# Moving one expert's scatter matmuls within the expert loop of a sparse mixture-of-experts stage

## What is computed

```
gate = ...                      # [256 tokens, 16 experts], two entries of a row are not zero
out = zeros_like(t)             # t: [256, 1024]
for e in range(16):
    hid = silu(t @ w1[e]) * (t @ w3[e])      # w1, w3: [1024, 512]
    out = out + gate[:, e:e+1] * (hid @ w2[e])   # w2: [512, 1024]
```

## Time and profile before

| what | value |
|---|---|
| median of 3 runs | 1847.81 us (1847.75 to 1850.71) |
| the profiled execution's own time | 1842.55 us |
| its span, first to last instruction | 1840.6 us |
| the expert loop in it | about 1494 to 1829 us |
| one pass of the loop | 20.97 us |

### The profile page before, as it was taken

How to read it: one execution, slowest core, us unless ns; L and a number is a source line. 1 busy time by engine, 2 the same in 40 slices (tenths; PEclk the granted TensorE clock), 3 DMA queues, 4 the chain that set the end, 5 groups by cost and what they waited for, 6 DMA issues and landing times.

```text
span 1840.6 us, 20850 instructions
## 1 busy us (share of the span) xinstructions
PE 1717.3 (93%) x8330; PEld 1370.4 (74%) x8330; DVE 1145.0 (62%) x1626; ACT 900.1 (49%) x1380; POOL 39.3 (2%) x45
## 2 busy tenths in 40 slices
PE   7999999999999999899999999979899879999997
PEld 7987886768887898697676788737658557777776
DVE  7366656565555836665756545554644378888887
ACT  5476433434443548543333444242532257777774
POOL 0010000000000001000000000001000000000000
PEclk9999999999999999999999999999956889999999
DMA  6454234446553545424554555362400248887885
GB/s 262 160 190 153 92 140 158 183 160 241 191 186 137 205 139 205 160 92 155 191 192 160 195 187 189 132 270 78 168 1 28 72 180 299 307 306 294 302 294 188
DMA packets 48746, 333.18 MB, mean 181 GB/s; under 512 B 6146, under 2 KB 6788, under 8 KB 9860
## 3 DMA queue, kind: packets, MB, share of 16 engines
q1 hardware_dynamic: 48644, 331.79, 49.0%
HBM read 330.72 MB, written 1.05 MB: 180 GB/s over the span
## 4 chain that ended last, share of the span: by engine, by line
PE 74%; DVE 15%; ACT 7%; DMA 2%; issue 1%; POOL 1%; DVEq 0%; SPq 0%; ACTq 0%
PE bank L192 71%; DVE wls L204 6%; PE bank L196 3%; ACT whs L200 2%; DMA raw<-in_ws_dram 2%; DVE arena L204 1%; DVE tail L209 1%; ACT tail L200 1%; DVE P0l L204 1%; ACT P0h L200 1%; DVE more L204 1%; ACT arena L201 1%; POOL sm L224 1%; ACT arena L200 1%; DVE arena L713 1%
## 5 line engine op out<-in xcount | busy, mean ns | idle before, releaser
L204 DVE TENSOR_TENSOR wls<-raw,whs 128x1024 fp32r<-128x1024 f32 x500 | 593.6, 1227 | 298.8 <-ACT whs L200 298.6
L200 ACT ACTIVATE whs<-raw 128x1024 fp32r<-128x1024 f32 x500 | 502.7, 1051 | 276.7 <-PE bank L192 197.0
L192 PE MATMUL bank<-whs,P0h 128*128 128x512 f32 (+1 forms) x1104 | 438.5, 397 | 29.1 <-DVE P0l L204 19.5
L192 PE MATMUL bank<-whs,P0l 128*128 128x512 f32 (+1 forms) x1104 | 429.3, 389 | 0.0
L192 PE MATMUL bank<-wls,P0h 128*128 128x512 f32 (+1 forms) x1104 | 428.6, 388 | 0.0
L192 PEld LDWEIGHTS bank<-whs,P0h 128*128 128x128 f32 x1104 | 208.9, 189 | 79.4 <-DVE P0l L204 22.8
L192 PEld LDWEIGHTS bank<-whs,P0l 128*128 128x128 f32 x1104 | 208.6, 189 | 44.1
L192 PEld LDWEIGHTS bank<-wls,P0h 128*128 128x128 f32 x1104 | 209.2, 189 | 40.0
L192 PE MATMUL bank<-whs,P1h 128*128 128x512 f32 x400 | 160.9, 402 | 6.1 <-DVE P1l L204 5.4
L192 PE MATMUL bank<-P0h,whs 128*128 128x256 f32 x512 | 148.5, 290 | 10.2 <-DVE P0l L204 6.1
L192 PE MATMUL bank<-whs,P1l 128*128 128x512 f32 x400 | 157.5, 394 | 0.0
(11 more groups left out here) (185 smaller groups left out, 1879.4 us busy)
## 6 DMA issues: line engine op xcount, KB each, us to landing
raw<-in_ws_dram SPq DMA_DIRECT2D x302, 1024.0 KB, 4.8
lnb<-in_ln_g_dram SPq DMA_DIRECT2D x6, 512.0 KB, 5.7
lnb<-in_ln_b_dram SPq DMA_DIRECT2D x6, 512.0 KB, 6.6
tail<-in_bias_dram SPq DMA_DIRECT2D x1, 2048.0 KB, 7.6
h<-in_x_dram SPq DMA_DIRECT2D x2, 512.0 KB, 3.9
lnb<-in_mem_dram SPq DMA_DIRECT2D x1, 1024.0 KB, 12.6
memT<-in_ctx_dram SPq DMA_DIRECT2D x1, 1024.0 KB, 7.0
lnb<-in_b_ada_dram SPq DMA_DIRECT2D x2, 512.0 KB, 9.6
```

The costliest lines, as they stand in the source:

```text
L192: return PE.put(lambda e: e.matmul(out, lhsT, rhs, start=start, stop=stop, skip_group_check=skip), w, inc)
L200: return AC.put(lambda e: e.activation(out, in_, func, bias=bias, scale=scale), w)
L204: return VE.put(lambda e: e.tensor_tensor(out, a, b, op), w)
```

## The change

The call `scatter(e - 1)` is moved from behind `down(e, 1)` to between `down(e, 0)` and `turn_hidden(e, 1)`. Nothing is added or taken away; for e = 0 there is no such call.

```
@@ expert loop @@
                 up(e, 1)
                 feed(1)
                 down(e, 0)
+                if e:
+                    scatter(e - 1)
                 turn_hidden(e, 1)
                 feed(1)
                 if e + 1 < NEXP:
                     pick(e + 1)
                 feed(1)
                 down(e, 1)
                 feed(1)
-                if e:
-                    scatter(e - 1)
                 if e + 1 < NEXP:
                     turn_onehot(e + 1)
```

## The result

The changed kernel is slower: 1858.76 us median (1856.81 to 1866.56, 6 runs) against 1847.76 us before (6 runs), a ratio of 1.0081 with a 95% interval of 1.0063 to 1.0099. (The ratio is that of the comparison of the timed runs and not the quotient of the two medians, which lie 11.0 us or 0.6% apart; 1.0081 is 15.0 us on 1847.76. The ratios further down are of the same kind, each against its own runs of the kernel before.) The forecast was 1851.0 us in a range of 1846.3 to 1856, within 0.2% of before the likeliest. The time lies outside the range, and a wait that the prediction doesn't name made it so.

The account below looks back on a forecast made before the run. PE bounds the loop, with DVE having only some 2.5 us to spare. Terms -3.5 + 3.5 + 2.4 + 0.8 = +3.2 us on 1842.55 us profiled, plus 5.3 to the median, gave 1851.0 us, range 1846.3 to 1856.

Parts of the forecast that it names:

- Term 1: PE's wait for P0l ahead of the second down product, counted from T (chunk 1 transposes' start), shrinks 0.25 us: -3.5 us.
- Term 2: New wait ahead of the next expert's u1 matmuls, 0.17 us idle plus 0.08 restart, 14 times: +3.5 us.
- Term 3: d0's landing delays P0l of chunk 0 and the next first down product, 0.17 us in 14 passes: +2.4 us.
- rival C: Slower: d0's landing at ACT's F3' lacks cover; 1854.5 us at 5.1 us, 1860.1 at 5.5; chance 0.23.
- Term 4: In the last pass the previous expert's scatter no longer covers part of the last Y split: +0.8 us.
- B: Gain without new waits: u1 closed by T + 7.65, only term 1 and the end count, 1845.1 us; chance 0.12.
- D: No visible effect: terms 1 and 2 cancel, landing 0.1 early, only the end counts, 1848.6 us; chance 0.15.

Follow-up runs that it names:

- the first experiment: Changed kernel with the first up product in PSUM bank 6 instead of bank 4 and the one-hot work in bank 7; ratio 1.0057 to the kernel before.
- after_swap: Changed kernel with the second down product making its two column halves in the order 1, 0; ratio 1.0221 to the kernel before.
- half: Kernel before with only the first 4 of the 8 scatter matmuls moved ahead of the chunk 1 transposes; ratio 1.0012.
- mid: Kernel before with the scatter between the chunk 1 transposes and the second down product, inside the wait for P0l; ratio 0.9942.
- before_bank: Kernel before, scatter in its old place, with the first up product in bank 6 and the one-hot work in bank 7; ratio 0.9992.
- after_bank: Same kernel as the first experiment: changed kernel with the first up product in bank 6 and one-hot work in bank 7; ratio 1.0057.

## Why the prediction was wrong

**Term 1** (P0l's wait 0.25 shorter) was right: 1.02 for 1.26, at T + 1.40. In all it came to 2.8 us instead of 3.5, since two passes had 1.02 or 1.03 already before.

**What was left out**, and made the prediction wrong, is a wait ahead of the next expert's first up product, which the prediction put at nothing without a reason. Term 2 says of u1: "Without the scatter and the 0.25 that is T + 7.65". This lets the u0 matmuls ahead of it start 2.1 us earlier than before, as soon as the one-hot work is through. The prediction asked whether the scatter hides the hidden values, and whether it waits itself. It looked at what the scatter's neighbours read, and not at where they write. The first up product writes bank 4, and bank 4 is released by the first Y split, at T + 6.09, by a DVE list that is rigid from F8 on. Before, PE wanted it at T + 6.91. After, it wants it at T + 4.79 (0.58 behind the start of the one-hot work, as before). All numbers for this stood in the trace of before. The prediction also read "19.5 us in 16 waits, all for P0l" as all that PE waits for, and passed over the row below it, the 0.88 us for Y0l in the pass without a scatter. The 1.30 us from T + 4.79 to T + 6.09, in 14 passes, are some 18 us. Less what term 1 gave, that is 15 us, and the 14 passes of the two profiles take 309.42 us against 294.02, 15.4 more (a typical one 1.01, the two longer ones about 1.3). What lies ahead of these passes in the loop, and behind them, adds 1.2. Terms 2 and 3, 5.9 us of the sum, were not paid on top, since PE was held already. The ratio gives 15 us; the spans differ by 14.3, with a loop that starts 2.3 us earlier.

The Trainium skill, page Perfetto Trace Analysis, section Matmuls, says that independent matmul groups should rotate through different PSUM banks so that the reading of one overlaps the next group's matmuls. The trace agrees: with a bank of its own for the first up product the 1.15 us are gone.

**Term 2** (u1, 0.25 later) didn't show in the changed kernel, since the bank held PE longer than u1 would have. It showed to 0.01 us once the bank was out of the way.

**Term 3** (d0 and P0l of chunk 0) likewise: hidden in the changed kernel, at T + 16.44 in the first experiment. Mis-sized was what follows it, a second failure that the bank's wait hid. The prediction said of d1's transfer that its halves "are wanted by the second down product only". On ACT the SiLU of chunk 1 is queued behind F5', so its landing also holds bank 5 and with it the second half of the first down product: 0.2 us more per pass, and over 1 us with a late landing. With the bank out of the way the ratio is 1.0057, which on 1847.76 us is 1858.3: term 3 with its consequences would alone have led out of the range. Half of the longer passes of that profile are rival C's, with d0 landing late, and half have d1 in the place of d0.

**Term 4** (the end) was right: DVE's final work starts at T + 5.64 instead of T + 6.76 while the scatter's 1.85 us were paid ahead of T, +0.7 (0.8 forecast).

**The rivals.** B is out: once the bank is free, u1's wait is there. C's mechanism shows in four passes of the first experiment, and is not what made the changed kernel slow: transfers of half the size leave it at 1.0093. D is what the kernel does with bank and landings both removed. What PE stood at in the changed kernel was in none of them. The two losses hide each other: with the bank's wait alone the ratio is 1.0093, with the landings alone 1.0057, with both (the changed kernel) 1.0081, with neither 0.9999.

## What to carry to other kernels

When an instruction group is moved away from in front of another, ask of the one behind it not only when its inputs come but when its output bank (or buffer) is read out: the moved work may have been the time in which that happens. A group that depends on nothing new is worth most where PE waits for a short round trip through ACT and DVE; there the same 1.85 us of scatter gained 0.6%, and 0.9% once bank and feed order allowed it. Put a figure to each cover before it is taken away: here 0.83 us for the bank, 2 us for u1, 0.4 us for d0. And look for a pass of the loop that lacks the group already, as that of e = 0 does here: it shows in the trace of before what its absence costs.

## What the runs showed of the hardware that was not expected

The granted clock of TensorE fell to 0.50 (its 1.2 GHz level) for about 3 us after a wait of 1.75 us that followed one of 1.02 us, with 3.5 us of matmuls between the two, in 12 of 14 passes of `after_swap`, and cost 1.6 us each time. With 1.15 in place of 1.75 (the changed kernel) it stayed at 1.00 throughout the loop. Two passes of `after_swap` with waits of the same length kept 1.00, so the length of the wait alone doesn't settle it.

Passes with a late landing come as the 4th and the 11th of the loop in the kernel before, the changed one, `half` and `mid`. In both it is the transfer of d1 that takes longer, 6.0 to 6.4 us from issue to landing where 4.7 to 4.9 is usual. From the one to the other are 147 us in the kernel before, 155 in the changed one and 142 in `mid`, so what recurs goes with the place in the stream of weights rather than with the time. It is not fixed: in `before_bank` the 4th takes the usual 4.8. How many late ones there are beyond these differs from profile to profile: 6 more in that of `after_bank`. That they cost little where a transfer has cover is shown by the passes; what makes a landing late stays open.
